# Attention streams of a two-block network on one core: units of a tile over query tiles 3, 0, 2, 1

## Chip, cores, metric

The kernel runs on 1 core of one Trainium2 chip. The metric is the device time in microseconds of one execution.

## What is computed

The input is one sequence of 512 tokens of width 1024 (float32). The layers are, in order: nsa attention, a gated conv feed-forward, swa attention, a second feed-forward, a norm, the even mixer, an MLP, the odd mixer, a second MLP, and the final norm. The four attentions differ in which keys a block of 128 queries sees:

```python
# nsa (16 heads, 4 kv groups): o = g0*compressed + g1*selected + g2*window; window and selection are causal here
m_w = (dist >= 0) & (dist < WINDOW_A) & (wpos[None, :] >= 0)          # WINDOW_A = 512
# swa (16 heads, 2 kv groups): own block of 128 and the one before, with a sink per head
mask = band[None] & exists
p = e / (e.sum(axis=-1, keepdims=True) + jnp.exp(sink - mx))
# even (8 heads, 2 kv groups): keys with |i - j| <= 128, with a sink
valid = (jnp.abs(kpos - qpos) <= A_WINDOW) & (kpos >= 0) & (kpos < S)
# odd (8 heads): dense, all 512 keys
p = jax.nn.softmax(s, axis=-1)
```

With 512 tokens all 8 selection blocks of 64 are taken, so the selected branch is causal attention over all keys, as the window branch is.

## The kernel before

All activations lie in SBUF with the features on the partitions. A product in full precision is made of three matmuls with operands split in a high and a low part (`product`, L519 to 523). Weights come in units of 1 MB that SyncE loads into two buffers; ScalarE writes the high part (`w_hi`, L958 by way of `copy`), VectorE the low part (`w_lo`, L1402). These projections take most of the time of TensorE (PE).

Between the projections of a mixer and its output projection stands an attention stream, which every engine runs from its own `attend` (PE L652, ScalarE L1094, VectorE L1582). The streams of nsa, swa, even and odd have 8, 8, 4 and 4 tiles; a tile is a pair of heads over all 512 queries. A tile is made of units: one for each query tile of 128 queries, in nsa two (the selected and the window branch). `attention_units` (L433) gives the list of units, and its order is the order on all engines. `key_blocks` (L438) says how many blocks of 128 keys a unit sees, its width:

| stream | query tile 0 | 1 | 2 | 3 |
|---|---|---|---|---|
| nsa | 1 | 2 | 3 | 4 |
| swa | 1 | 2 | 2 | 2 |
| even | 2 | 3 | 3 | 2 |
| odd | 4 | 4 | 4 | 4 |

The stream is a software pipeline, written out in steps s:

- PE: scores of unit s into X (L594), its masks (L599); transposes of the probabilities of unit s-2 into D (L607); products with the values of unit s-3 (L615). At the first unit of an nsa tile come the compressed values (L649).
- VectorE (DVE): negated row maximum of unit s (L1593); the sink column of unit s+1 in swa and even (L1579); reciprocal of the sum and scaling of unit s-1 (L1603, L1608 or L1610); copy of the second head's transposed probabilities of unit s-2 from D (L1619); at steps 4 after a tile's last unit the low part of the tile's output (the helper's line L1402).
- ScalarE (ACT): copy of the first head's transposed probabilities of unit s-2 (L958), exponentials of unit s (L1116), at the end of a tile the high part of its output (L958).

There are two buffers each of X, `prob` and `prob_t`, but one of D for the transposes. So scores of unit s wait for the exponentials of unit s-2 (in swa and even for their sink column, which is written after these), and transposes of unit n wait for the scaling of unit n and for both copies of unit n-1 (L666 to 670). The projection behind a stream begins when the low part of the last tile is done (L695). GpSimd and the DMA queues have no part in a stream.

Of the kernel before, what the change touches and what calls it, by code (L numbers as in the profile page):

```python
# [28 lines left out]
QT = SEQ // P  # L29
# [51 lines left out]
TILES = {"nsa": 8, "swa": 8, "even": 4, "odd": 4}  # L81
# [74 lines left out]
def build_program(nc, d, layers=LAYERS):  # L156
# [3 lines left out]
    with ExitStack() as ctx:  # L160
# [271 lines left out]

        def attention_units(kind):  # L433

            return [(t, qt, branch) for t in range(TILES[kind]) for qt in range(QT)
                    for branch in range(BRANCHES[kind])]

        def key_blocks(kind, qt):  # L438
# [78 lines left out]
        def _(pe):  # L517
# [134 lines left out]
            def attend(kind, l):  # L652

                units, a0 = attention_units(kind), units_before[l]
                count, per = len(units), QT * BRANCHES[kind]
                for s in range(count + 3):
# [296 lines left out]
        def _(act):  # L953
# [140 lines left out]
            def attend(kind, l):  # L1094
                units, a0 = attention_units(kind), units_before[l]
                count, per = len(units), QT * BRANCHES[kind]
                for s in range(count + 4):
                    if 0 <= s - 2 < count:

                        a = a0 + s - 2  # L1100
                        w = len(key_blocks(kind, units[s - 2][1])) * P
                        act.wait_ge(turned, a + 1)
                        if s >= 4:
                            act.wait_ge(pv_done, a - 1)
                        copy(prob_t[:, a % 2, 0, 0:w], D[:, 0, 0:w]).then_inc(evac_a, 1)
                    if s < count:
                        a = a0 + s
                        w = len(key_blocks(kind, units[s][1])) * P + (kind in SINK0)
                        par = a % 2
                        act.wait_ge(maxed, a + 1)  # L1110
                        if s >= 2:

                            act.wait_ge(turned, a - 1)
                        for o in range(2):
                            c = 2 * par + o
                            ins = nc.scalar.activation(prob[:, par, o, 0:w], X[:, c, 0:w], ACT.Exp,  # L1116
                                                       bias=neg_max[:, c:c + 1], accum_out=row_sum[:, c:c + 1])
                        ins.then_inc(exped, 1)
                    if s >= 4 and (s - 4) % per == per - 1:

                        t = (s - 4) // per
                        act.wait_ge(pv_done, a0 + s - 3)
                        copy(mid[:, t, 0, :], D[:, 2 + t % 2, :]).then_inc(ao_high, 1)
# [265 lines left out]
        def _(dve):  # L1389
# [191 lines left out]

            def attend(kind, l):  # L1582
                units, a0 = attention_units(kind), units_before[l]
                count, per = len(units), QT * BRANCHES[kind]
                if kind in SINK0:
# [678 lines left out]
```

## Time and profile before

| | |
|---|---|
| median of 3 runs | 2609.9 us (2609.86 to 2615.91) |
| profiled execution | 2609.84 us, of it the span of the profile 2608.0 us |
| PE busy | 2409.2 us (92%) |
| DVE busy | 1369.4 us (53%) |
| ACT busy | 923.9 us (35%) |
| POOL busy | 281.2 us (11%) |
| share of PE in the chain that ended last | 81% (DVE 13%, ACT 4%) |
| mean granted clock of PE | 0.962 of full speed |

Busy times of PE overlap and their ends are modelled, so the trace is read by starts: the time from one group's start to the next one's is the price of the first, if the second did not wait. A PEld row is a weight load, which precedes its matmul. "[0.56 <-DVE prob L1608]" says how long the engine sat idle before, and what ended that. PEclk 0.50 is 1.2 GHz, 1.00 is 2.4 GHz.

### The profile page before, as it was taken

How to read it: one execution, taken by the hardware profiler on the slowest of the kernel's cores; microseconds unless marked ns; L12 is line 12 of the kernel's file. 1: busy time of each engine (PE TensorE's matmuls, PEld its weight loads, DVE VectorE, ACT ScalarE, POOL GpSimd, SP SyncE). 2: the span in 40 equal slices, each digit the busy share in tenths (PEclk: the TensorE clock that was granted, in tenths of full speed). 3: DMA queues.
4: the chain of work that ended last, by engine and by line, in shares of the span. 5: the costliest groups of instructions: out<-in, count | busy, mean ns of one | idle time of the engine just before them, and what ended most of it. 6: DMA issues, size and time to landing. Idle time of an engine off the chain costs nothing.

```text
span 2608.0 us, 30433 instructions
## 1 busy us (share of the span) xinstructions
PE 2409.2 (92%) x11732; PEld 1872.0 (72%) x11732; DVE 1369.4 (53%) x1633; ACT 923.9 (35%) x1365; POOL 281.2 (11%) x188
## 2 busy tenths in 40 slices
PE   7988989999998889999998799999996789999997
PEld 6765557887876557887876567888875546788886
DVE  5446875664545565664536654333355655433333
ACT  4324653443323353442323343322225453332221
POOL 0000003110013003110000013110140000311010
PEclk9987999999999899999998899999998789999999
DMA  4310002222222102222222202222321101222231
GB/s 168 129 65 1 1 1 77 100 96 84 96 96 89 65 1 81 96 96 97 97 97 89 81 24 88 99 85 92 113 89 65 38 27 36 87 104 82 96 109 68
DMA packets 31204, 202.54 MB, mean 78 GB/s; under 512 B 4356, under 2 KB 5256, under 8 KB 7432
## 3 DMA queue, kind: packets, MB, share of 16 engines
q1 hardware_dynamic: 29816, 198.14, 21.5%
q10 hardware_dynamic: 1296, 3.15, 0.4%
q8 instruction: 62, 1.02, 0.2%
q14 instruction: 30, 0.25, 0.0%
HBM read 199.17 MB, written 2.10 MB: 77 GB/s over the span
## 4 chain that ended last, share of the span: by engine, by line
PE 81%; DVE 13%; ACT 4%; issue 2%; DMA 0%; ACTq 0%; DVEq 0%; SPq 0%
PE D L522 69%; PE X L594 3%; PE D L615 2%; PE D L607 2%; DVE neg_max L1593 2%; DVE w_lo L1402 2%; DVE xg L1427 1%; ACT w_hi L958 1%; PE X L599 1%; ACT prob L1116 1%; DVE mid L1402 1%; ACT mid L958 1%; PE X L560 1%; DVE h L1442 1%; DVE prob_t L1619 0%
## 5 line engine op out<-in xcount | busy, mean ns | idle before, releaser
L522 PE MATMUL D<-xg,w_hi 128*128 128x512 f32 x3184 | 992.8, 393 | 51.5 <-DVE xg L1427 29.4
L522 PE MATMUL D<-mid,w_hi 128*128 128x512 f32 x2312 | 731.7, 398 | 23.0 <-DVE w_lo L1402 9.2
L522 PEld LDWEIGHTS D<-xg,w_hi 128*128 128x128 f32 x3184 | 601.2, 189 | 182.8 <-DVE w_lo L1402 23.8
L1402 DVE TENSOR_TENSOR w_lo<-w_raw,w_hi 128x2048 fp32r<-128x2048 f32 x184 | 451.2, 2452 | 381.7 <-ACT w_hi L958 380.9
L522 PE MATMUL D<-xg,w_lo 128*128 128x512 f32 x1592 | 623.7, 392 | 0.0
L522 PEld LDWEIGHTS D<-mid,w_hi 128*128 128x128 f32 x2312 | 435.1, 189 | 134.1 <-issue 17.4
L958 ACT ACTIVATE w_hi<-w_raw 128x2048 fp32r<-128x2048 f32 x184 | 351.6, 1911 | 501.3 <-PE D L522 493.9
L522 PE MATMUL D<-mid,w_lo 128*128 128x512 f32 x1156 | 458.7, 397 | 0.0
L522 PEld LDWEIGHTS D<-xg,w_lo 128*128 128x128 f32 x1592 | 301.3, 189 | 63.6
L522 PEld LDWEIGHTS D<-mid,w_lo 128*128 128x128 f32 x1156 | 218.3, 189 | 53.0
L1442 DVE TENSOR_TENSOR h<-D,h 128x1024 f32 (+1 forms) x72 | 88.0, 1222 | 283.2 <-PE D L522 283.2
L1994 POOL TENSOR_TENSOR sq<-h 128x512 f32 x48 | 56.0, 1167 | 1106.4 <-DVE h L1442 1101.8
L1116 ACT ACTIVATE prob<-X,neg_max 128x512 f32<-128x512 f32 (+6 forms) x256 | 132.6, 525 | 47.7 <-DVE neg_max L1593 46.8
L1593 DVE TENSOR_REDUCE neg_max<-X 128x2 f32<-128x514 f32 (+6 forms) x128 | 105.2, 822 | 62.8 <-PE X L599 47.1
L1500 DVE SCALAR_TENSOR_TENSOR conv_out<-conv_in,vec,conv_out 128x512 f32<-128x512 f32 x176 | 124.2, 747 | 11.4 <-ACT conv_out L1033 6.4
L2020 POOL TENSOR_TENSOR mid<-mlp_u,mid 128x1024 f32 x32 | 77.1, 2408 | 451.7 <-ACT mid L958 451.7
L607 PE MATMUL D<-ident,prob 128*128 128x128 f32 x640 | 96.0, 282 | 21.1 <-DVE prob_t L1619 20.2
L2020 POOL TENSOR_TENSOR mid<-ffn_y,mid 128x512 f32 x44 | 56.8, 1292 | 522.4 <-ACT mid L958 522.4
L1046 ACT ACTIVATE mlp_u<-relu_z 128x1024 f32<-128x1024 f32 x32 | 33.9, 1060 | 220.6 <-DVE relu_z L1519 220.6
L1491 DVE TENSOR_TENSOR conv_in<-D,rstd_b 128x1024 f32<-128x1024 f32 x44 | 53.9, 1225 | 108.2 <-PE D L522 104.4
L958 ACT ACTIVATE prob_t<-D 128x256 f32<-128x256 f32 (+3 forms) x128 | 56.0, 438 | 125.9 <-PE D L607 125.9
L607 PEld LDWEIGHTS D<-ident,prob 128*128 128x128 f32 x640 | 71.6, 144 | 39.4 <-issue 14.6
(233 smaller groups left out, 1815.7 us busy)
## 6 DMA issues: line engine op xcount, KB each, us to landing
w_raw<-in_weights SPq DMA_DIRECT2D x184, 1024.0 KB, 4.8
h<-in_x SPq DMA_DIRECT2D x4, 512.0 KB, 7.8
out_y<-h SPq DMA_DIRECT2D x4, 512.0 KB, 2.7
inv_cnt<-in_inv_cnt ACTq DMA_DIRECT2D x1, 1024.0 KB, 4.8
cos<-in_cos ACTq DMA_DIRECT2D x3, 256.0 KB, 5.2
sin<-in_sin ACTq DMA_DIRECT2D x3, 256.0 KB, 5.8
vec<-in_vec SPq DMA_DIRECT2D x1, 262.0 KB, 2.7
cos<-in_cos_m ACTq DMA_DIRECT2D x1, 256.0 KB, 2.7
```

The lines of the kernel that those rows point to most:

```text
L522: last = nc.tensor.matmul(out, w[a], x[b], start=start and k == 0, stop=stop and k == 2)
L594: last = nc.tensor.matmul(X[:, 2 * par + o, 0:w * P], query_of(kind, t, o, qt), keys_of(kind, t, o, qt, branch), start=True, stop=not edge ...
L607: last = nc.tensor.transpose(D[:, o, span(j)], prob[:, a % 2, o, span(j)], ident[:, :])
L958: return nc.scalar.activation(out, in_, ACT.Copy, **more)
L1116: ins = nc.scalar.activation(prob[:, par, o, 0:w], X[:, c, 0:w], ACT.Exp, bias=neg_max[:, c:c + 1], accum_out=row_sum[:, c:c + 1])
L1402: return nc.vector.tensor_tensor(out, x, f(high), ALU.subtract)
L1442: nc.vector.tensor_tensor(tiles, D[:, 2 * s:2 * s + 2, :], tiles, ALU.add).then_inc(d_free[s], 1)
L1491: nc.vector.tensor_tensor(conv_in[:, par, :, 2:], D[:, 2 * s:2 * s + 2, :], by_rstd([P, 2, SEQ]), ALU.mult).then_inc(d_free[s], 1)
L1500: ins = nc.vector.scalar_tensor_tensor(out, conv_in[:, par, o, tap:tap + SEQ], vec[:, bass.ds(c, 1)], out, ALU.mult, ALU.add)
L1593: nc.vector.tensor_reduce(neg_max[:, c:c + 2], X[:, c:c + 2, 0:w], AX_X, ALU.max, negate=True).then_inc(maxed, 1)
L1994: link(nc.gpsimd.tensor_tensor(sq[:, :], h[:, t, :], h[:, t, :], ALU.mult))
L2020: nc.gpsimd.tensor_tensor(out, x, high.bitcast(F32), ALU.subtract).then_inc(mid_low, 1)
```

## The change

The list of units runs over the query tiles in the order 3, 0, 2, 1 in all four streams. The engines all read the list, so their steps stay matched. The tiles, the branches and the work of each unit are the same.

```diff
         def attention_units(kind):
 
-            return [(t, qt, branch) for t in range(TILES[kind]) for qt in range(QT)
+            return [(t, qt, branch) for t in range(TILES[kind]) for qt in (3, 0, 2, 1)
                     for branch in range(BRANCHES[kind])]
```

## Rows read from the trace of the kernel before

**Rows 1.** The page: the chain that ended last, share of the span by line

```profile
PE D L522 69%; PE X L594 3%; PE D L615 2%; PE D L607 2%; DVE neg_max L1593 2%; DVE w_lo L1402 2%; DVE xg L1427 1%; ACT w_hi L958 1%; PE X L599 1%; ACT prob L1116 1%; DVE mid L1402 1%; ACT mid L958 1%; PE X L560 1%; DVE h L1442 1%; DVE prob_t L1619 0%
```

**Rows 2.** Windows: stretch, us, busy PE, PEld, DVE, ACT, POOL, PEclk, DMA; streams, then tiles

```profile
215.08:387.33 172.25, 159.07 (x1376) 96.01 (x1377) 137.28 (x328) 100.81 (x328) 0.00 (x0) 0.97 0.01 1
891.22:968.86 77.64, 66.80 (x529) 39.11 (x529) 57.46 (x198) 44.77 (x168) 0.00 (x0) 0.93 0.01 3
1485.68:1534.97 49.29, 42.12 (x353) 26.09 (x353) 34.93 (x98) 26.40 (x84) 0.00 (x0) 0.89 0.01 5
276.53:297.12 20.59, 19.20 (x174) 11.74 (x173) 17.09 (x43) 12.57 (x42) 0.00 (x0) 1.00 0.01 2
911.72:920.53 8.81, 7.87 (x67) 4.62 (x67) 7.17 (x26) 5.59 (x22) 0.00 (x0) 1.00 0.01 2
1509.78:1520.28 10.50, 9.56 (x88) 6.02 (x89) 8.68 (x26) 6.60 (x22) 0.00 (x0) 1.00 0.00 1
```

**Rows 3.** Timeline, nsa stream, tile from 276.53: start, us, engine, line, op

```profile
285.17 1.07 PE L649 MATMUL D<-c_prob_t,vc_all 32*64 32x512 f32 x4
...
290.17 0.42 PEld L607 LDWEIGHTS D<-ident,prob 128*128 128x128 f32 x4 [0.79 <-DVE prob L1608]
...
291.34 1.13 PE L594 MATMUL X<-kdup,q_all 64*128 64x512 f32 x4
...
292.40 0.11 PEld L599 LDWEIGHTS X<-masks,ident_b 128*128 128x128 bf16 x2 [0.76 <-issue]
...
292.47 0.64 PEld L607 LDWEIGHTS D<-ident,prob 128*128 128x128 f32 x6
...
292.73 1.23 DVE L1593 TENSOR_REDUCE neg_max<-X 128x2 f32<-128x1024 f32 x1 [0.50 <-PE X L599]
...
293.87 0.16 DVE L1603 RECIPROCAL inv_sum<-row_sum 128x2 f32<-128x2 f32 x1
...
294.06 0.87 DVE L1608 TENSOR_SCALAR prob<-prob,inv_sum,gates 128x384 f32<-128x384 f32 x2
...
295.51 0.64 PEld L607 LDWEIGHTS D<-ident,prob 128*128 128x128 f32 x6 [0.47 <-issue]
...
296.31 0.64 PEld L615 LDWEIGHTS D<-prob_t,vall 128*64 128x64 f32 x12 [0.17 <-issue]
...
296.63 1.00 DVE L1608 TENSOR_SCALAR prob<-prob,inv_sum,gates 128x512 f32<-128x512 f32 x2
...
297.12 0.49 PE L594 MATMUL X<-kdup,q_all 64*128 64x128 f32 x4
...
297.54 0.11 PEld L599 LDWEIGHTS X<-masks,ident_b 128*128 128x128 bf16 x2
...
297.55 0.55 DVE L1619 COPY prob_t<-D 128x384 f32<-128x384 f32 x1
...
298.02 0.41 DVE L1593 TENSOR_REDUCE neg_max<-X 128x2 f32<-128x256 f32 x1
...
298.22 0.86 PEld L607 LDWEIGHTS D<-ident,prob 128*128 128x128 f32 x8 [0.56 <-DVE prob L1608]
...
299.24 0.63 PEld L615 LDWEIGHTS D<-prob_t,vall 128*64 128x64 f32 x12 [0.17 <-issue]
...
299.46 0.68 DVE L1619 COPY prob_t<-D 128x512 f32<-128x512 f32 x1
```

**Rows 4.** Timeline, start of the nsa stream, low clock

```profile
217.59 1.22 PE L594 MATMUL X<-kdup,q_all 64*128 64x256 f32 x4 [0.30 <-ACT prob L1116]
```

**Rows 5.** Windows: granted clock in the first us of the nsa and odd streams

```profile
224.00:227.00 3.00, 3.00 (x16) 1.55 (x14) 0.94 (x2) 0.09 (x1) 0.00 (x0) 0.54 0.00 0
227.00:230.00 3.00, 2.97 (x24) 1.55 (x23) 2.77 (x9) 2.42 (x9) 0.00 (x0) 1.00 0.00 0
...
2122.00:2125.00 3.00, 3.00 (x5) 1.20 (x4) 1.22 (x1) 0.34 (x1) 0.00 (x0) 0.57 0.00 0
```

**Rows 6.** Timeline, swa stream: scores that wait for the sink column

```profile
911.72 0.70 PE L594 MATMUL X<-kd,q_all 64*128 64x256 f32 x4 [0.40 <-DVE X L1579]
```

## The prediction

> **What bounds the kernel now.** The chain that ended last comes first: 69% of it is the projection matmuls of L522, which the change does not touch [rows 1]. The lines of the attention streams (L594, L599, L607, L615, L1593, L1116, L1619) share the rest. So the windows come next. The nsa stream takes 172.3 us, the swa stream 77.6, the even stream 49.3 [rows 2]. The odd stream is left out, since every unit of it sees all four key blocks and the order of its query tiles changes no width. What can move is 299 us, 11% of the span. In a tile of the nsa stream PE is busy 19.20 of 20.59 us and DVE 17.09 [rows 2]: PE is the bound, and waits for DVE now and then. So the tile is read in order of time, and the question is how long PE waits in it.
>
> **The change.** No instruction is added or removed: each tile still has its units of 1, 2, 3 and 4 key blocks (nsa, each twice), 1, 2, 2, 2 (swa) or 2, 3, 3, 2 (even). Only the neighbours change: nsa goes from 1 1 2 2 3 3 4 4 to 4 4 1 1 3 3 2 2, swa to 2 1 2 2, even to 2 2 3 3. No DMA is issued in the streams, so no queue is moved past. In step s PE does scores(s), masks(s), transposes(s-2), values(s-3); DVE does reduce(s), reciprocal and scaling(s-1), copy(s-2), and after the fourth step of a tile the low part of the tile before. The transposes wait for the copy of the unit before, because they write the bank that it reads. So PE's transposes(s-1) wait for the whole of DVE's step s.
>
> **Prices, from start to next start, for b key blocks [rows 3].** Scores: 1.06 at b=4 (291.34 to 292.40), 0.42 at 1 (297.12 to 297.54), so 0.20+0.215b. Masks 0.07. Transposes: 0.81 at 3 (292.47), 1.02 at 4 (298.22 to 299.24), so 0.16+0.215b; values the same (0.81 at 296.31). Compressed values, once a tile, about 1.0 (busy 1.07). DVE: the reduce starts 0.33 after the masks (292.40, 292.73), and takes 1.14 at 4 to the next start, 0.33 at 1 (busy 0.41 less the 0.08 overlap); reciprocal 0.19; scaling 0.79 at 3, 0.92 at 4, so 0.65 at 2 and 0.52 at 1; copy to its end 0.55 at 3, 0.68 at 4, so 0.42 and 0.28; from there 0.12 to PE (298.10 to 298.22).
> PE's sum for an nsa tile: 60 block passes (3 kinds, 20 blocks) x 0.215 = 12.9, eight steps x (0.20+0.07+0.16+0.16) = 4.7, plus 1.0: 18.6 us. The tile takes 20.59, so PE waits 2.0 us. The rows show where: at 290.17 (reached at 289.33: 0.84), 295.51 (reached at 295.00: 0.51) and 298.22 (reached at 297.61: 0.61), 1.96 in all.
>
> **The new nsa tile laid out with these prices.** Units 4a 4b 1a 1b 3a 3b 2a 2b, t=0 at scores(4a).
> Step 4a: DVE reduces from 1.38, scales 2b and copies 2a until 3.80. PE does transposes(2a), values(3b), scores(4b) and masks until 3.65, and waits until 3.92: 0.27.
> Step 4b: DVE from 3.90: 1.14+0.19+0.92+0.42, done 6.57. PE meanwhile has only transposes(2b) 0.59, values(2a) 0.59, scores(1a) and masks 0.49: it is there at 5.59 and waits until 6.69: 1.10. This is the largest stall, the widest DVE work over the narrowest PE work.
> Steps 1a, 1b: PE has transposes(4a), (4b), the compressed values and values(4a), DVE only small reduces. No wait, but transposes(4b) clear by only 0.05. The low part (0.69) falls here and is hidden; before, it came in a step of width 2 with little cover.
> Step 3a: no wait, by 0.09. Step 3b: DVE from 15.31: 0.86+0.19+0.79+0.28, done 17.43. PE has transposes(1b), values(1a), scores(2a), there at 16.50, waits until 17.55: 1.05. Step 2a: 0.18.
> The waits are 2.60 us, the tile 21.2: 0.6 us longer. Ends: if the two sites with PE narrow cost 0.15 less each, +0.3; if the two thin margins fail by as much, +0.9. I take 0.6.
> The stream: tile 2 gains 0.4 and the five after it 0.6 each: +3.3. The first tile runs mostly at the low clock, where scores of two blocks take 1.22 us busy and not 0.70 [rows 4]: a block costs 0.43, not 0.215. In the five steps that the old order had at low clock (until about 227 [rows 5]) it had 9 blocks of scores, 4 of transposes, 2 of values; the new one has 13, 9 and 8. The 15 more cost 6.4 us there and save 3.2 later: +3.2, and 3.1 when laid out with fill. The end: the last two units are 2 wide, not 4. From the start of the last tile to the projection it was 28.4 us (387.33 less 297.12 less three tiles of 20.59 [rows 2, 3]); laid out, 26.8: -1.6. Sum for nsa +4.8.
> One term against this: the clock. In the odd stream, all units 4 wide, the clock reads 0.57 already in the window 2122 to 2125, some 5 us after the stream began; nsa's start took 11.6 [rows 5]. With 4 4 first nsa could be like odd. At most this returns the 3.2 us, at least nothing; nsa's PE was busy from 218 on and the clock still stayed low, so I take 0.9. nsa: +3.9.
> The Trainium skill's page "TensorE: Matmul & The Clock Gate", section "What's actually happening", says the throttled clock is the default and PE activity lifts it. By that rule the wide start is lifted earlier and the term is the whole 3.2; the trace agrees on the direction with the odd row, and does not fix the size.
>
> **swa.** PE's loop is scores, masks, reduce, sink column, next scores: scores at 911.72 wait 0.40 for the sink [rows 6]. Behind the low part the first reduce is now 2 wide and not 1 (0.60 for 0.33), so the next scores come 0.28 later; the narrow unit behind it gives part back. Per tile 0 to +0.27, taken 0.12: seven tiles +0.8, start +0.25. **+1.1**, from 0 to 2.1.
> **even.** First tile -0.8 (2 wide, not 3, behind the first unit at low clock). Then 3 3 stand together at the tile's end, and the copies of both come in the two steps with short PE work: +0.3 in each of two tiles, and the last tile ends on 3 and not on 2: +1.0. **+0.8**, from -0.5 to 1.5 (1.5 is the 49.3 us stream with 0.3 in each tile and the end).
>
> **Sum.** 3.9+1.1+0.8 = 5.8. The profiled execution took 2609.84 us (span 2608.0 and 1.8 around it), the median of three runs is 2609.9: 2615.6. A measurement tells about 0.3%, 7.8 us, from no change, so the forecast is within 0.3%, a small loss.
>
> **Rivals.** *The mix evens the load (faster).* Next to a narrow unit a wide one leaves the busier engine slack; if all waits of nsa's PE went, 8 x 1.96 = 15.7 us, 2594. Against it: the layout, in which wide units still stand in pairs and the waits only move. For it: ACT and the pairs of equal width give each engine more than one step of slack. 4%.
> *The clock comes back early.* As in the odd stream [rows 5], with the whole 3.2 us back: nsa +1.6, and swa and even, whose first unit is no narrower than before, 0.5 less each. Sum 1.6+0.6+0.3 = 2.5: 2612.4. Still within 0.3%. 18%. The rule of the Trainium skill's page named above makes this the case to expect.
> *No effect.* The waits of a tile only change place, and fill and drain cancel: 2610. 8%.
> *The clock comes back later (slower).* The streams swa and even start 5 us later than before, and at their starts PE is half idle in the loop over the sink, so the clock may stay low longer than it did. Three more us at the low clock in each of the three streams cost 1.5 each, 4.5 in all: 2620. It decides above 2.0 us more than my sum, so with two of three streams hit. For it: nothing in the rows but the 11.6 us that nsa needed. With it goes the case that the two thin margins fail (0.3 x 7 = 2.1). 16%.
> The forecast, 2615.6, has 54%; its own range is 2613 to 2618.
>
> **Numbers.** The range is 2610.5 to 2620: from no effect to the slow rival. Of the forecast's 54% some 5 lie above 2617.7, and a few of the slow rival's below. Faster by over 0.3%: 4%. Within: 77%. Slower: 19%.
>
> **What would show it.** nsa tiles of 21.2 us in the windows (20.59 now); PE's longest waits at transposes of the second unit, behind the copy of L1619, with 4 4 on DVE and 1 on PE, 1.1 us, and one of 1.05 behind 3 3; none behind 1 1. The nsa stream near 176 us, swa 78.7, even 50.1. The first window in which nsa's clock reads 1.00: before 224 means the clock rival. The forecast is wrong if the tile is under 20.3 or over 21.6 us, or if a stage outside the streams moves by over 1 us.

## The result, and the profile after

| | before | after |
|---|---|---|
| median | 2610.2 us (6 runs, 2609.9 to 2615.9) | 2629.2 us (6 runs, 2622.7 to 2631.9) |
| profiled execution | 2609.84 us, span 2608.0 | 2627.44 us, span 2625.6 |
| mean granted clock of PE | 0.962 | 0.957 |
| instructions | 30433 | 30433 |

The ratio is 1.0064, with a 95% interval from 1.0047 to 1.0081: slower by 0.64%, some 17 us. The forecast was 2615.6 us and its range ended at 2620.

From the page of the kernel after (busy us and share of the span, then the clock in 40 slices, then the chain by line):

```profile
PE 2419.6 (92%) x11732; PEld 1879.3 (72%) x11732; DVE 1370.5 (52%) x1633; ACT 924.0 (35%) x1365; POOL 281.2 (11%) x188
...
PEclk9987999999999899999998899999999789999999
...
PE D L522 68%; PE X L594 4%; PE D L615 3%; PE D L607 3%; DVE w_lo L1402 2%; DVE neg_max L1593 1%; DVE xg L1427 1%; ACT w_hi L958 1%; PE X L599 1%; PE X L690 1%; PE D L632 1%; PE X L560 1%; DVE h L1442 1%; DVE mid L1402 0%; ACT mid L958 0%
```

DVE's busy time rose by 1.1 us and PE's by 10.4 [2409.2 before], with the same instructions. The same work that is busy for longer on PE alone points at its clock. It does not exclude the waits, in which PE is not busy. The chain has the same shape [rows 1].

Windows of the kernel after: the streams of nsa, swa and even, then one nsa tile (columns as in rows 2):

```profile
217.73:397.79 180.06, 162.40 (x1377) 97.71 (x1377) 138.81 (x328) 100.72 (x328) 0.00 (x0) 0.95 0.01 1
904.46:984.51 80.05, 66.69 (x528) 39.69 (x529) 56.92 (x198) 44.74 (x168) 0.00 (x0) 0.92 0.01 3
1502.78:1552.32 49.54, 41.25 (x353) 25.45 (x353) 34.95 (x98) 26.60 (x84) 0.00 (x0) 0.92 0.01 5
307.06:328.31 21.25, 19.37 (x176) 11.78 (x174) 17.29 (x42) 12.58 (x42) 0.00 (x0) 1.00 0.01 2
```

The tile takes 21.25 us and the clock in it is full; the forecast had 21.2. Cutting both spans at the first scores of each stream and the first projection matmul behind it gives, in us:

| stretch | before | after | difference | forecast |
|---|---|---|---|---|
| start to the nsa stream | 215.1 | 217.7 | +2.6 | 0 |
| nsa stream | 172.2 | 180.1 | +7.8 | +3.9 |
| to the swa stream | 503.9 | 506.7 | +2.8 | 0 |
| swa stream | 77.6 | 80.1 | +2.4 | +1.1 |
| to the even stream | 516.9 | 518.3 | +1.4 | 0 |
| even stream | 49.3 | 49.5 | +0.3 | +0.8 |
| from there to the end | 1073.0 | 1073.3 | +0.3 | 0 |

The waits of PE in the nsa tile from 264.56, from the timeline of the kernel after (start, us, engine, line, op):

```profile
268.14 0.28 PE L599 MATMUL X<-masks,ident_b 128*128 128x128 bf16 x2
268.49 0.63 PE L607 MATMUL D<-ident,prob 128*128 128x128 f32 x4
...
270.05 0.28 PE L599 MATMUL X<-masks,ident_b 128*128 128x128 bf16 x2
271.28 1.06 PE L607 MATMUL D<-ident,prob 128*128 128x128 f32 x8 [0.94 <-DVE prob_t L1619]
...
281.02 0.28 PE L599 MATMUL X<-masks,ident_b 128*128 128x128 bf16 x2
282.18 0.85 PE L607 MATMUL D<-ident,prob 128*128 128x128 f32 x6 [0.88 <-DVE prob_t L1619]
283.32 0.70 PE L594 MATMUL X<-kdup,q_all 64*128 64x256 f32 x4
283.96 0.28 PE L599 MATMUL X<-masks,ident_b 128*128 128x128 bf16 x2
284.22 0.84 PE L607 MATMUL D<-ident,prob 128*128 128x128 f32 x6
```

From the masks plus 0.07 to the transposes PE stands still for 0.28, 1.16, 1.09 and 0.19 us, 2.72 in all. The layout said 0.27, 1.10, 1.05 and 0.18, 2.60 in all. The start of the stream is another matter. Windows of the kernel after, its first 18 us:

```profile
217.73:220.73 3.00, 3.00 (x8) 1.14 (x10) 0.56 (x1) 0.00 (x0) 0.00 (x0) 0.50 0.00 0
220.73:223.73 3.00, 2.54 (x11) 0.71 (x8) 1.89 (x3) 1.45 (x4) 0.00 (x0) 0.50 0.00 0
223.73:226.73 3.00, 2.17 (x11) 1.63 (x10) 2.57 (x8) 1.45 (x4) 0.00 (x0) 0.50 0.00 0
226.73:229.73 3.00, 3.00 (x17) 2.33 (x18) 1.81 (x6) 1.31 (x6) 0.00 (x0) 0.50 0.00 0
229.73:232.73 3.00, 3.00 (x16) 1.39 (x18) 0.68 (x1) 1.28 (x5) 0.00 (x0) 0.50 0.00 0
232.73:235.73 3.00, 3.00 (x26) 1.66 (x24) 0.64 (x1) 0.28 (x1) 0.00 (x0) 0.71 0.00 0
```

PE runs at 1.2 GHz (0.50) until about 234.4, for 16.7 us of the stream and not for 11.6 as before [rows 5]. The first tile takes 25.58 us; before it took 20.15. (Later traces with the old order have 13.6 to 13.9 us and 20.8 to 20.9, so the usual difference is 3.1 and 4.7.) And behind the streams the projection starts at the low clock too. Windows of the kernel after, behind nsa and behind swa:

```profile
397.79:400.79 3.00, 3.00 (x8) 2.40 (x9) 0.00 (x0) 0.00 (x0) 0.00 (x0) 0.59 0.00 0
400.79:403.79 3.00, 3.00 (x12) 2.36 (x12) 0.00 (x0) 0.00 (x0) 0.00 (x0) 0.84 0.00 0
984.51:987.51 3.00, 3.00 (x9) 2.38 (x10) 0.00 (x0) 0.00 (x0) 0.00 (x0) 0.65 0.00 0
987.51:990.51 3.00, 3.00 (x12) 2.40 (x11) 0.00 (x0) 0.00 (x0) 0.00 (x0) 0.78 0.00 0
```

and of the kernel before, behind nsa:

```profile
387.33:390.33 3.00, 3.00 (x13) 2.45 (x14) 0.00 (x0) 0.00 (x0) 0.00 (x0) 1.00 0.00 0
```

The same matmuls of L522: 8 records in three us where there were 13. The two low windows behind nsa are worth 3 x (0.41+0.16) = 1.7 us of work at full clock.

### The profile page after: what moved, and what is told of

Same layout as the page of the kernel before. It is cut to its first block, busy times and chain, and to the rows that moved or that the text cites. A ratio compares the mean times of both kernels' runs of the same rounds, so it can differ in the third digit from the quotient of the medians.

```text
span 2625.6 us, 30433 instructions
## 1 busy us (share of the span) xinstructions
PE 2419.6 (92%) x11732; PEld 1879.3 (72%) x11732; DVE 1370.5 (52%) x1633; ACT 924.0 (35%) x1365; POOL 281.2 (11%) x188
## 3 DMA queue, kind: packets, MB, share of 16 engines
q1 hardware_dynamic: 29816, 198.14, 21.2%
## 4 chain that ended last, share of the span: by engine, by line
PE 82%; DVE 12%; ACT 4%; issue 2%; DMA 0%; ACTq 0%; DVEq 0%; SPq 0%
PE D L522 68%; PE X L594 4%; PE D L615 3%; PE D L607 3%; DVE w_lo L1402 2%; DVE neg_max L1593 1%; DVE xg L1427 1%; ACT w_hi L958 1%; PE X L599 1%; PE X L690 1%; PE D L632 1%; PE X L560 1%; DVE h L1442 1%; DVE mid L1402 0%; ACT mid L958 0%
## 5 line engine op out<-in xcount | busy, mean ns | idle before, releaser
L522 PE MATMUL D<-xg,w_hi 128*128 128x512 f32 x3184 | 992.3, 393 | 51.8 <-DVE xg L1427 29.3
L522 PE MATMUL D<-mid,w_hi 128*128 128x512 f32 x2312 | 736.1, 400 | 21.5 <-DVE w_lo L1402 7.7
L522 PEld LDWEIGHTS D<-xg,w_hi 128*128 128x128 f32 x3184 | 600.6, 189 | 183.2 <-DVE w_lo L1402 24.9
L522 PE MATMUL D<-xg,w_lo 128*128 128x512 f32 x1592 | 622.7, 391 | 0.0
L522 PEld LDWEIGHTS D<-mid,w_hi 128*128 128x128 f32 x2312 | 438.0, 190 | 133.7 <-issue 17.5
L958 ACT ACTIVATE w_hi<-w_raw 128x2048 fp32r<-128x2048 f32 x184 | 351.6, 1911 | 505.1 <-PE D L522 496.9
L522 PE MATMUL D<-mid,w_lo 128*128 128x512 f32 x1156 | 461.1, 399 | 0.0
L522 PEld LDWEIGHTS D<-xg,w_lo 128*128 128x128 f32 x1592 | 301.1, 189 | 63.5
L522 PEld LDWEIGHTS D<-mid,w_lo 128*128 128x128 f32 x1156 | 219.7, 190 | 53.5
L1593 DVE TENSOR_REDUCE neg_max<-X 128x2 f32<-128x1024 f32 (+6 forms) x128 | 105.3, 823 | 69.7 <-PE X L599 53.5
```

The lines of the kernel that those rows point to most:

```text
L522: last = nc.tensor.matmul(out, w[a], x[b], start=start and k == 0, stop=stop and k == 2)
L958: return nc.scalar.activation(out, in_, ACT.Copy, **more)
L1593: nc.vector.tensor_reduce(neg_max[:, c:c + 2], X[:, c:c + 2, 0:w], AX_X, ALU.max, negate=True).then_inc(maxed, 1)
```

## The experiments

**How the runs are compared.** Medians stand beside ratios, which weigh all executions. Each execution's span and mean clock give its low-clock time: 2 x (1 - clock) x span us at 1.2 GHz. The clock is on record to three digits, which is 5 us of low-clock time, so only means over several executions tell something. Half of that is the price of the low clock if PE was the bound in it, and the span less that half is what the kernel would take at full clock. Over six runs the kernel after has 228 us at the low clock and 2511.8 without its price; the kernel before has 208 and 2506.2 (19 runs). By this account the order costs 5.6 us by its work, and 20 more us at the low clock cost 10. This split is an estimate; the runs below test it. It can't see a longer wait that lies in a low stretch. The kernel before had a median of 2610.8 us beside the first four runs and 2614.6 beside the others (its single times gather near 2610 and near 2615), so small differences are read from ratios and from the streams.

The first two runs take the change apart (only the loop over the query tiles in `attention_units` is shown).

```diff
-for qt in range(QT)
+for qt in ((3, 0, 2, 1) if kind == "nsa" else range(QT))     # e1_nsa_only
+for qt in ((3, 0, 2, 1) if kind != "nsa" else range(QT))     # e2_swa_even_only
```

> The order 3, 0, 2, 1 in the nsa stream alone, the other streams as before. The changed kernel's profiled execution was 17.6 us longer: 7.8 in the nsa stream, 2.4 in swa, 0.2 in even, and 7.2 in stages whose instructions and order did not change. Theory A (clock): the order costs 0.65 us in each full nsa tile (5 us in all with fill and end) and, because PE's work begins in other places, low-clock stretches of other length in and behind the stream. Then nsa alone gives most of it: +8 to +13 us, tiles of 21.2 us, and a spread of several us between executions. Theory B (work alone, as I had summed it): +3.9 to +4.8 us with little spread. Theory C (each stream pays in proportion to its length): +10.

> The order 3, 0, 2, 1 in swa and even (and odd, where it changes nothing), nsa as before. Theory A: swa and even cost 2.4 and 0.2 us as in the changed kernel, and the clock behind them decides the rest: +2 to +6 us. Theory B: +1.9. If it gives over +8, the nsa stream is not where the loss comes from.

Measured: nsa alone 2618.8 us, ratio 1.0028 (1.0018 to 1.0039), low-clock time 211 us, the rest 2512.3. The others alone 2624.1 us, 1.0040 (1.0028 to 1.0051), low-clock time 231 us, the rest 2505.4. The two add up to the whole, 0.68 against 0.64%. They are of different kinds: by the split nsa costs work (+6.1 us, almost no more low clock), swa and even cost no work that shows and 23 us of low clock. The expectations were met in part. The nsa run's 7.3 us by the ratio are above "work alone" (3.9 to 4.8), but hardly from more low clock, as theory A had it. The other run's 0.40% are 10.4 us, where theory A had 2 to 6 and work alone 1.9: over half of the loss is not in nsa. In the trace of the second, steady swa tiles of 9.01 us stand beside two of 10.54.

The next two hold the clock: 48 matmuls of 384 columns on PE ahead of each stream, with the old and the new order. Their own time is in both.

```diff
+for _ in range(48):
+    nc.tensor.matmul(D[:, 0, 0:3 * P], ident_b[:, :], masks[:, :, :].rearrange("p m c -> p (m c)"),
+                     start=True, stop=True)
```

> The order as before, with 48 extra matmuls (128 by 384, bf16, of constants, into a bank that the stream overwrites) on PE ahead of each of the four streams, so that every stream starts at the full clock. They cost time themselves (48 x 0.16 us at 2.4 GHz, double at 1.2 GHz, 8 to 15 us each), so it is compared with the next run, stream by stream. Expected in the trace: nsa stream from the first scores to the projection 169 us (172.3 less about half of the PE work of the 11.6 us at low clock), swa 75, even 46.5.

> The same extra matmuls with the order 3, 0, 2, 1. Against the run before it: theory A (the excess over my sum is the low clock) wants the difference to fall to that of the layout with no low clock: nsa +4.8, swa +1.1, even +0.9, in all +6 to +7 us. Theory B' (the order itself costs 17 us by work and waits) wants +14 or more.

Measured: 2641.6 us (1.0114) with the old order and 2652.6 (1.0152) with the new one, 11.0 apart. The mean clock of nsa, even and odd is 1.00 in both, that of swa 0.98 and 0.96. nsa takes 168.9 and 174.4 us with the clock at 1.00 throughout: +5.5, made of six tiles at +0.65 (3.9), the end at -1.5 and the first tile at +3.1. The forecast had the first two as +3.3 and -1.6, so these were sized right. It had +3.1 for the first tile too, but for blocks that cost more at the low clock. Here that tile is as much longer with no low clock at all. First tiles of the nsa stream, old order, then new:

```profile
226.01:242.87 16.86, 14.80 (x114) 7.81 (x113) 13.35 (x34) 9.75 (x35) 0.00 (x0) 1.00 0.00 1
227.44:247.38 19.94, 16.61 (x139) 9.56 (x138) 14.82 (x35) 10.52 (x35) 0.00 (x0) 1.00 0.00 1
```

Of the 3.1 us 1.8 are PE work that comes sooner and is missing at the end of the stream; the rest is waiting. In swa the difference is 4.0, of which 1.5 is a tile of 10.55 us with the clock at 0.84: the clock falls in the middle of the stream, though it had been lifted ahead of it. In even it is 1.1. So the 11.0 us lie between the two cases expected (6 to 7, and 14 or more), and swa is the stream that was priced too low.

To see that better, swa alone, and swa alone with every transpose done twice (which adds 14 matmuls to a tile).

```diff
-for qt in range(QT)
+for qt in ((3, 0, 2, 1) if kind == "swa" else range(QT))     # e5_swa_only and e6_swa_twice
...
-for j in range(len(key_blocks(kind, unit[1]))):
+for j in list(range(len(key_blocks(kind, unit[1])))) * (2 if kind == "swa" else 1):     # e6_swa_twice
```

> The order 3, 0, 2, 1 in the swa stream alone. In the trace of swa and even together the swa tiles were 9.01 us (8.80 before), but two of them 10.54, and in those the granted clock fell to half in the middle of the stream; before, no tile behind the start did that. Theory A (the new order gathers PE's waits of a tile, PE falls idle enough for the clock to drop): swa alone gives most of the +11 of that run: +7 to +11 us, again with tiles of 10.5 at a clock under 1.00. Rival (the even stream and what follows it is as guilty): swa alone +2 to +5.

> As the run before, but in the swa stream every transpose is done twice (the same result written again), so PE has 56 block passes more (12 us of work and some 5 of fixed cost), part of which falls into its waits. If PE's idle time is what makes the clock drop (theory A), no tile behind the start shows a clock under 1.00 and all tiles have one length, between 9.6 and 11; the time is 5 to 14 us over the run before less the dips that are gone. If the dips come from something else (the time of the stream, chance), tiles of two lengths, 1.5 us apart, stay.

Measured: 2617.6 us, 1.0021 (1.0010 to 1.0032), low-clock time 224 us (214 in the kernel before beside it); with more work 2617.1 us, 1.0018 (1.0009 to 1.0028), low-clock time 205 us. Swa alone costs 5.5 us by the ratio and 3.0 by the medians. That is not the 7 to 11 that theory A had, and near the 2 to 5 of its rival: against the run with both (10.4 us by the ratio), even and what follows it add about as much. Windows of the swa stream alone, in the first of them (stream; two tiles; three windows in a third tile):

```profile
896.97:983.13 86.16, 72.76 (x528) 43.37 (x529) 57.01 (x198) 44.60 (x168) 0.00 (x0) 0.84 0.01 3
934.92:943.93 9.01, 7.72 (x68) 4.61 (x67) 7.07 (x26) 5.58 (x22) 0.00 (x0) 1.00 0.01 3
943.93:954.48 10.55, 9.20 (x69) 5.51 (x67) 7.08 (x26) 5.58 (x22) 0.00 (x0) 0.84 0.00 0
...
915.80:917.80 2.00, 0.75 (x8) 0.41 (x6) 1.96 (x8) 1.11 (x5) 0.00 (x0) 1.00 0.00 0
917.80:919.80 2.00, 1.96 (x14) 1.34 (x15) 1.31 (x6) 1.08 (x5) 0.00 (x0) 0.59 0.04 8
919.80:921.80 2.00, 2.00 (x10) 1.23 (x10) 0.36 (x1) 0.00 (x0) 0.00 (x0) 0.56 0.00 0
```

and in the second:

```profile
897.96:982.90 84.94, 75.33 (x641) 51.19 (x641) 57.67 (x198) 44.54 (x168) 0.00 (x0) 0.96 0.01 3
935.50:945.39 9.89, 9.04 (x83) 6.19 (x82) 7.17 (x26) 5.57 (x21) 0.00 (x0) 1.00 0.00 1
```

DVE's columns are the same in the two tiles of the first kernel; only PE's clock differs. In the window before the fall PE is busy for 0.75 of 2 us while DVE is busy for 1.96. The reason is in the timeline of that kernel, here two tiles further on: scores of the narrow unit wait 0.87 us for the sink column, and the transposes behind them wait again.

```profile
946.80 0.49 PE L594 MATMUL X<-kd,q_all 64*128 64x128 f32 x4 [0.87 <-DVE X L1579]
947.94 0.63 PE L607 MATMUL D<-ident,prob 128*128 128x128 f32 x4 [0.43 <-DVE prob_t L1619]
```

In the old order the two waits (0.40 at 911.72 [rows 6] and 0.38 at 918.91) lie 7.2 us apart, and no two us between 913 and 945 show PE busy for less than 1.22. With 14 matmuls more in each tile, all five steady tiles take 9.89 us at full clock, less than the 10.54 of the tiles in which the clock fell. The kernel with 112 more matmuls is not slower, and 19 us of low clock are gone, in the means of 10 and 12 executions. The fastest executions tell what the matmuls cost where few falls are saved: 2616.3 with them, 2612.8 without. So the low clock in mid-stream goes when PE is given work in its idle time, and by the split it carries most of the price of the order in swa (10 us more of it, 5 us, against 1 of work).

How often the clock falls is not fixed. Of the five steady swa tiles in each of seven traces with the new order (after, e2, e4, e5, e9, e10, e11) 0, 2, 1, 4, 0, 3 and 1 take 10.5 us, 11 of 35; of 20 in four traces with the old order (before, e1, e3, e8) none. The falls have a fixed place: the two waits of a tile end 2.9 and 4.0 us after its first scores, and all eleven falls begin 3.9 to 4.9 us after them. The last tile has the same two waits, and in after, e2, e5 and e9 the clock falls in it at the same place. So each of the seven traces has such a fall, and that of the doubled transposes has none. The tile without the fall waits in the same way, 9.01 us with PE busy for 7.72. So in these traces the fall comes only behind the gathered waits, but they don't decide it alone. What else does is open.

The next two look for the gain on the other side: the narrow unit last, and the old order with extra matmuls where PE idles ahead of the streams (20 to 30 at a time, before the waits of `compressed_turn`, of the last `query_swap` and of `attend`; `masks` as the operand, into a buffer that is written anew).

```diff
-for qt in range(QT)
+for qt in {"nsa": (1, 3, 2, 0), "swa": (1, 2, 3, 0), "even": (1, 2, 0, 3), "odd": (0, 1, 2, 3)}[kind]     # e7_narrow_last
```

```diff
+def keep_busy(out, n):     # e8_keep_busy
+    for _ in range(n):
+        nc.tensor.matmul(out[:, 0:3 * P], ident_b[:, :], masks[:, :, :].rearrange("p m c -> p (m c)"),
+                         start=True, stop=True)
...
+if n == 3:
+    keep_busy(D[:, 2 * (at["q"] % 2), :], 26)
 if n >= 2:
     pe.wait_ge(q_ready, qpairs_before[l] + n - 1)
...
+keep_busy(D[:, 2 * (at["q"] % 2), :], 30)
 pe.wait_ge(q_ready, qpairs_before[l] + 4)
 attend("swa", l)
```

> Another order, chosen with the same layout that gave 21.2 for the changed nsa tile: nsa 1, 3, 2, 0 (widths 2 4 3 1), swa 1, 2, 3, 0 (2 2 2 1), even 1, 2, 0, 3 (3 3 2 2). Laid out: nsa tile 20.2 (20.6 before), swa 8.7 (8.8), even 10.3 (10.5), and a short end; streams -3.7, -1.0 and -0.5 us. If the layout carries and the low clock is no longer than before: 2605 us, -5. If the clock decides, anything from -8 to +8 with the low-clock time showing it.

> The order as before; extra matmuls (128 by 384, bf16, of constants) only where PE stands idle ahead of the streams: 26 behind the third swap of the queries, 30 behind the fourth in swa and even, 20 in each of three waits between the compressed groups in nsa, 20 ahead of the odd stream; into banks that nobody reads. Theory A: with PE busy there the streams start at the full clock and the low-clock time falls by 40 to 80 us of some 208; at half price, and since part of it lay in waits, -8 to -20 us. If the low clock at the starts costs nothing (PE would wait for DVE anyway), no change or a loss of 1 to 5 us where the extra matmuls overhang.

Measured: narrow last 2604.6 us, ratio 0.9965 (0.9951 to 0.9978), 9 us where the layout had 5. Kept busy 2599.4 us, 0.9944 (0.9931 to 0.9956), with 134 us of low clock for the 214 of the kernel before beside it. Windows with the narrow unit last (nsa, swa, even, one nsa tile):

```profile
219.05:386.11 167.06, 157.41 (x1377) 95.52 (x1377) 137.89 (x328) 100.36 (x328) 0.00 (x0) 0.98 0.01 1
892.81:968.25 75.44, 65.41 (x529) 38.51 (x529) 56.84 (x198) 44.47 (x168) 0.00 (x0) 0.93 0.01 3
1485.86:1534.11 48.25, 41.81 (x353) 26.00 (x353) 34.95 (x98) 26.22 (x84) 0.00 (x0) 0.90 0.01 5
280.42:300.62 20.20, 19.26 (x175) 11.79 (x173) 17.20 (x42) 12.53 (x43) 0.00 (x0) 1.00 0.00 1
```

The tile is 0.4 us shorter than before, as laid out, and the last tile with the drain takes 24.9 us, not 28.4. With PE kept busy the streams of swa and even are at full clock from start to end (74.23 and 46.01 us, were 77.64 and 49.29 [rows 2]); nsa is not helped (173.12).

The last four put the pieces together: the changed kernel again; the new order in every tile but the first of each stream (`(3, 0, 2, 1) if t else range(QT)`); and PE kept busy as above with the new order, and with the narrow unit last.

> The changed kernel once more, unaltered, beside new runs of the kernel before. If its extra low clock belongs to the order, the median is again 2622 to 2632 us, 12 to 17 above the kernel before, with a mean clock of 0.955 to 0.958, and steady nsa tiles of 21.25 us; the first nsa tile may be 22 or 25.6. If the low clock of the first trace was that chip's, the median is 2614 to 2618 (order alone, 5.6 us) with a clock of 0.960 to 0.962.

> Order 3, 0, 2, 1 in every tile but the first of each stream, which keeps the order 0 to 3. If the wide units at a stream's start cost the low clock there (forecast term +3.2, seen as 25.6 us for the first nsa tile), the first nsa tile is 20.2 to 20.9 us, the nsa stream 175 to 176, and the median 3 to 5 us below the changed kernel's. If the low clock at the start comes from the execution and not from the order, the two medians differ by under 1.5 us. In both cases swa keeps its dips.

> The extra matmuls of the run with the kernel kept busy (2599.4 us, low-clock time 134 us), now with the order 3, 0, 2, 1. If the order costs its laid-out work alone, once the streams start at the full clock: +5.6 us, 2605, low-clock time unchanged at 134, swa tiles 9.01 throughout, swa stream 75.3. If the gathered waits of PE drop the clock in the middle of the stream even then: some swa tiles of 10.5, the stream 78 to 81, low-clock time 145 to 155, the median 2609 to 2615.

> The same extra matmuls with the orders of the run that puts the narrow unit last (nsa 1, 3, 2, 0; swa 1, 2, 3, 0; even 1, 2, 0, 3). The two gains are in different places, so they should add: nsa 167.1, swa 72.7 (eight tiles of 8.64 and a start and an end shorter by 1.3), even 45.2, the median 2599.4 - 8 = 2591 us, 0.990 to 0.992 of the kernel before. If the full clock at the starts already gives most of the gain of the narrow-last order, 2597 to 2599.

Measured: 2629.5 us, ratio 1.0064 (1.0049 to 1.0079), low-clock time 230 us, first nsa tile 25.65: the result repeats, to the figure. First tile old: 2620.5 us, 1.0033 (1.0020 to 1.0046), low-clock time 219 us; the first nsa tile 20.86, the second (whose neighbour is then 4 4) 22.63, the stream 176.8 for 180.1. So 3.3 us of nsa's loss hang on the order of its first tile. They are not all the clock's. With the clock held that tile was 3.1 us longer at full clock too, and 1.4 us of this come back here in the second tile; so about half of the 3.3, an estimate, is the low clock. By the medians the gain is 9 us, more than the 3 to 5 expected; its swa stream (83.7) had three tiles of 10.5 even so, its profiled execution (2628.1) was one of its slowest, and the rest is not accounted for.

Kept busy with the new order: 2616.9 us, 1.0012 (1.0001 to 1.0023). That is 17.5 above the same fill with the old order (17.3 by the spans of the traces: nsa +7.1, swa +5.3, even +3.6, the rest +1.3), so the case in which the order costs 5.6 us once the streams start at full clock falls, and the other was priced too low by 2 us. In nsa that case was not tried, since the fill doesn't lift the clock there; swa and even, at 8.9 us for a forecast of 1.9, decide it. Windows at the start of swa and in its middle, in this kernel:

```profile
893.90:896.90 3.00, 1.92 (x12) 0.97 (x11) 2.85 (x5) 0.00 (x0) 0.00 (x0) 1.00 0.83 300
896.90:899.90 3.00, 1.67 (x12) 0.83 (x12) 1.21 (x4) 1.20 (x6) 0.00 (x0) 0.89 0.13 49
899.90:902.90 3.00, 2.92 (x12) 1.82 (x14) 1.79 (x9) 0.79 (x5) 0.00 (x0) 0.50 0.00 0
...
933.90:936.90 3.00, 1.71 (x18) 1.23 (x18) 2.93 (x13) 1.40 (x7) 0.00 (x0) 0.98 0.00 0
936.90:939.90 3.00, 3.00 (x18) 1.63 (x14) 1.11 (x5) 0.80 (x5) 0.00 (x0) 0.50 0.00 0
```

and with the old order:

```profile
885.90:888.90 3.00, 1.91 (x12) 0.97 (x11) 2.85 (x5) 0.00 (x0) 0.00 (x0) 1.00 0.81 273
888.90:891.90 3.00, 2.14 (x16) 1.13 (x16) 1.69 (x6) 1.37 (x7) 0.00 (x0) 1.00 0.18 76
891.90:894.90 3.00, 2.37 (x20) 1.23 (x16) 2.22 (x8) 1.75 (x7) 0.00 (x0) 1.00 0.00 0
```

Both enter the stream at 1.00 after the same three us. PE is then busy for 1.67 us in the new order, whose first unit is two blocks wide and keeps the reduce and the sink column longer, and for 2.14 in the old one. The clock falls in the first and stays in the second, in one trace each.

Kept busy with the narrow unit last: 2594.3 us, ratio 0.9931 (0.9918 to 0.9944), the fastest kernel of this study, 0.69% below the kernel before. Its streams take 166.6, 73.0 and 45.4 us. The two gains would add to 0.91%; the streams do add (8.4 us below the same fill with the old order), but the medians are only 5.0 apart, for the 8 expected. In the traces the stretches between the streams took 6.5 us more. Part of that is the choice of execution, since the profiled one (2597.5) is 3.2 above its median, and part is the clock: the trace has 144 us of it low, for 136, with 3.4 us right behind swa. The rest was not tried.

## Why the prediction was wrong

The step that failed is the clock. The sum let it change only at the start of nsa, where it took 0.9 us off, priced swa and even almost by their layout alone (1.9 us together), and put "Stages outside the streams" at 0. The runs show in its place a clock that falls in more places with the new order: by the ratios nsa alone costs 7.3 us, swa and even 10.4, and these two come with 23 us more at the low clock. A smaller failure is in nsa's first tile, where +3.1 stood for 4.7 measured.

One trace of each kernel says too little of where it goes, since the low stretches differ from one execution to the next, and the trace of before is of its fastest one. Means over all traces without extra matmuls, by the order of the stream in front or at hand (before, after, e1, e2, e5, e6, e9, e10; e6 not for swa, e10 not for nsa):

| stretch | old order, us | new order, us | difference | forecast |
|---|---|---|---|---|
| nsa stream | 172.9 (4 traces) | 178.9 (3) | +6.0 | +3.9 |
| from nsa to swa | 505.1 (4) | 506.2 (3) | +1.2 | 0 |
| swa stream | 77.5 (2) | 82.6 (5) | +5.1 | +1.1 |
| from swa to even | 516.8 (2) | 517.6 (5) | +0.8 | 0 |
| even stream | 48.8 (4) | 50.5 (4) | +1.7 | +0.8 |
| from even to the end | 1073.0 (4) | 1073.9 (4) | +0.9 | 0 |

They add to 15.7 us, near the 17 of the ratio. In the streams the two orders don't overlap; in the stretches between them they do, so these differences are weak. Swa is the largest miss: it takes 80.0 to 86.2 us, and the trace of after is at the low end.

- **Layout of the steady tile, right.** 21.25 us against 21.2, with the four waits at their places. swa's tile costs 0.20 more (9.01), inside 0 to 0.27 but above the 0.12 taken. In even the steady tile costs 0.37 more (10.87 for 10.50) and the last one with the drain 1.3, for 0.3 and 1.0; the stream costs 1.1 us at full clock, forecast +0.8.
- **The end of nsa, right.** 26.99 us against 26.8.
- **The first tile of nsa, right by luck in one part and wrong in the other.** Its +3.1 was worked out as 15 more blocks at the low clock, 6.4 us there, less 3.2 saved later. The saving is counted twice. Only 7 of the 15 blocks are caught up within that tile (1.5 us); the other 8 are those that the end of the stream has less, and its -1.6 counts them again. By its own prices the term was 4.9. Measured are 4.7 over the usual 20.9 in three of four traces (25.6 in after, e9, e11). The runs with the clock held show what it is made of: 3.1 is the order at full clock (19.94 for 16.86), and the clock comes back after 16.8 us for 13.6 to 13.9, which is 3.1 us at half price, 1.5.
- **The clock term of nsa's start, wrong in sign in three of four traces.** The step said that the wide start could bring the clock back early and took 0.9 us off. In the fourth (e1) it did: the clock reads 1.00 from 221.5 to 224.9 and from 228.3 on, 10.1 us of the stream are low, and the tile takes 22.1. What decides between the two is open. The odd stream was a poor witness: at the start of nsa PE stands still for DVE (busy 2.54 and 2.17 of 3 us in the windows from 220.73), which "busy from 218 on" passed over.
- **"Stages outside the streams: 0", wrong for the clock, not shown for the time.** The clock is low for the first us of the projection behind nsa in all six traces with the new order in nsa (after, e1, e4, e9, e10, e11: 0.54 to 0.63 and 0.80 to 0.89), and at 1.00 in the six with the old one (before, e2, e3, e5, e6, e8). It is low with the narrow unit last too (e7, 0.57 and 0.86), so it is not the mark of this order alone. It is worth 1.7 us. But with the old order the clock is low once some 50 us further on, in all of these but before, and from nsa to swa it took 505.4 or 505.5 us in e2, e5, e6 and e8, and 503.9 only in the trace of before; with the new order it took 505.3 and 505.2 in e1 and e10, 506.7 in the others. What in the end of the stream makes the clock fall is not shown; the busy share of the last three us is alike in both (1.28 and 1.30).
- **The clock inside a stream, left out.** The forecast let it be low at starts only. The falls in the middle and at the end of swa (its last tile with the drain takes 17.5 us in the kernel after, 18.1 and 18.2 in e5 and e2, 15.8 before) are the largest part of what the order costs there. That they also make the time of the kernel spread, 9 us over its six runs, is likely, but was not shown.
- **The 2.6 us ahead of nsa are no effect of the order.** Four other traces have the stream's start at 218.5 to 219.2 with the old order in nsa or in its first tile (e2, e5, e6, e10); before's 215.1 came from the clock at 0.90 in 185 to 189, where after's reads 0.50.
- **The rival "the clock comes back later"** had the right sign, and at nsa's start the right size: 3.1 us more, 1.5. But at the starts of swa and even in the trace of after the clock came back no later than in that of before. The same price came up in swa's middle and at its end, which no rival had. "Evens the load" fell; that an order could even it was true of another order.

The Trainium skill's page "TensorE: Matmul & The Clock Gate", section "What's actually happening", was weighed in the forecast for a clock that is lifted earlier by a wide start. Three of four traces did not bear that out, and one did. Its section "HAM oscillation — how this bites in real kernels" tells of a kernel whose clock falls in every long wait for data. Here it fell inside tiles whose longest single wait was 0.87 us, so a long wait is not needed for it; the measurement decides.

## What to carry to other kernels

An order of units that leaves the sum of work alone is priced twice: by the waits of a steady tile, which a layout from start to start gives to a tenth of a us, and by how the waits gather on TensorE, since its clock can fall there and cost more than the wait: 1.5 us a time in swa, where the waits of a tile grew by 0.2. So look in the windows of before for the stretches in which PE is least busy at full clock, and ask whether the change deepens them. Where much low clock stands ahead of short stages, idle-time matmuls and the narrowest unit at the end of a stream are cheap to try: here 0.56 and 0.35%.

## What the runs showed of the hardware

- TensorE's clock fell in the middle of a stream in 11 of 35 tiles with the same instructions and waits, each time behind the two waits of the tile (0.87 and 0.43 us), and cost 1.5 us each time. A tile without the fall has PE busy for 7.72 of 9.01 us.
- More work made no difference to the time: swa with all its transposes doubled took as long as without (2617.1 and 2617.6 us), as 19 us of low clock went.
- Extra matmuls in the idle time of PE took the low-clock time from 214 to 134 us, and 0.56% off the time.
